# The value projection moved ahead of the key projection, and the key rotation's draining ticks set between query and key products of the recurrence

## The reference

```python
h = modulate(x, norm1_gain, sh1, sc1);  z = h @ w_in
gq, gk, gv, gr, glr, dq, dk, dv, gates = split(z)
# mixer A: gated linear attention, 4 heads, state 128 x 256, blocks of 16 tokens, decay from glr
# mixer B: differential attention, 8 heads; q and k: rmsnorm per 64 values, then rotary
qd = rope(rmsnorm(dq, q_gain), pos);  kd = rope(rmsnorm(dk, k_gain), pos);  v = dv
x = x + gt1 * ((sigmoid(g_a) * y_a + sigmoid(g_b) * y_b) @ w_out)
h2 = modulate(x, norm2_gain, sh2, sc2)
# PEER: per token 8 heads x 16 experts chosen by top-k of product keys among 16384
act = gelu(sum(h2 * peer_u[idx]));  x = x + gt2 * sum(g * act * peer_v[idx])
```

## Time and profile before

| | |
|---|---|
| median of three runs | 4257.27 us |
| profiled execution, its own time | 4264.31 us |
| its span | 4262.5 us |
| mean granted clock of TensorE | 0.802 |
| PE matmul / weight load / DVE / ACT / POOL busy | 73% / 47% / 64% / 35% / 29% |
| DMA | 1499.19 MB, mean 352 GB/s |

### The profile page before, as it was taken

One profiled execution on the slowest core, in us unless ns is written; L12 is line 12 of the kernel. 1 busy time (PEld: TensorE's weight loads), 2 busy tenths in 40 slices (PEclk: granted clock), 3 DMA queues, 4 the chain that ended last, 5 costly groups with the idle time before them and its releaser, 6 DMA issues. The chain is left out here.

```text
span 4262.5 us, 48896 instructions
## 1 busy us (share of the span) xinstructions
PE 3112.3 (73%) x15864; PEld 1989.7 (47%) x15864; DVE 2708.3 (64%) x7617; ACT 1513.0 (35%) x3085; POOL 1253.3 (29%) x1068
## 2 busy tenths in 40 slices
PE   6787688898788769788887679788776676633333
PEld 4676565676555327555554347454442364400000
DVE  1326357437667884578568874596678845776775
ACT  3533366312255651113555540133456611010010
POOL 0000112112233332333233332333333323354453
PEclk8798888899888779899878789888787788855555
DMA  7485767788989989999889899999999999999997
GB/s 263 142 323 188 285 237 260 270 312 336 361 342 373 359 313 398 394 417 404 352 353 361 335 368 385 414 399 400 382 387 383 373 414 413 396 415 415 414 404 329
DMA packets 269366, 1499.19 MB, mean 352 GB/s; under 512 B 44969, under 2 KB 81673, under 8 KB 97465
## 3 DMA queue, kind: packets, MB, share of 16 engines
q0 software_dynamic: 152064, 1107.36, 65.1%
q1 hardware_dynamic: 117048, 388.70, 24.2%
HBM read 1463.49 MB, written 31.36 MB: 351 GB/s over the span
## 5 line engine op out<-in xcount | busy, mean ns | idle before, releaser
L1711 POOL DMA_INDIRECT rt_ring<-in_peer_uv,rt_few_idx x1056 | 1250.0, 1184 | 2979.8 <-PE rt_acc L886 2344.6
L1657 DVE SCALAR_TENSOR_TENSOR rt_ring<-rt_ring,rt_h 128x1024 f32<-128x1024 f32 x1056 | 1267.6, 1220 | 541.2 <-DMA rt_ring<-in_peer_uv,rt_few_idx 536.6
L886 PE MATMUL rt_acc<-rt_ring,rt_diag 128*32 128x512 f32 x4224 | 762.4, 797 | 602.3 <-DVE rt_diag L1668 600.4
L635 PE MATMUL pair<-dense,w 128*128 128x256 f32 (+2 forms) x3056 | 599.4, 355 | 25.8 <-DMA w<-in_weights 24.2
L635 PEld LDWEIGHTS pair<-dense,w 128*128 128x128 f32 x3056 | 518.2, 198 | 140.7 <-issue 62.9
L624 PE MATMUL pair<-w,dense 128*128 128x256 f32 (+1 forms) x2352 | 557.8, 395 | 7.0 <-DVE dense L1313 2.8
L1212 ACT ACTIVATE rt_act_dot<-rt_dot 128x2 f32<-128x2 f32 x528 | 106.0, 202 | 1271.7 <-DVE rt_ring L1657 1262.5
L886 PEld LDWEIGHTS rt_acc<-rt_ring,rt_diag 128*32 128x32 f32 x4224 | 100.9, 122 | 930.1 <-DVE rt_diag L1668 789.3
L624 PEld LDWEIGHTS pair<-w,dense 128*128 128x128 f32 (+1 forms) x2352 | 437.5, 189 | 159.1 <-issue 73.7
L1668 DVE TENSOR_SCALAR rt_diag<-cst,rt_act_dot,rt_few_prob 128x32 f32<-128x32 f32 x1056 | 266.2, 297 | 82.6 <-ACT rt_act_dot L1212 64.1
L635 PE MATMUL bank<-dense,w 128*128 128x256 f32 (+2 forms) x1424 | 276.0, 350 | 1.4 <-DMA w<-in_weights 0.9
(11 more groups left out here) (241 smaller groups left out, 3314.5 us busy)
## 6 DMA issues: line engine op xcount, KB each, us to landing
w<-in_weights SPq DMA_DIRECT2D x284, 1024.0 KB
rt_ring<-in_peer_uv,rt_few_idx POOLq DMA_INDIRECT x1056
dense<-scratch_mod SPq DMA_DIRECT2D x18, 512.0 KB, 11.0
dense<-in_x_prompt SPq DMA_DIRECT2D x16, 512.0 KB, 10.3
rt_h<-scratch_h SPq DMA_DIRECT2D x33, 128.0 KB
rt_x<-scratch_x SPq DMA_DIRECT2D x132, 32.0 KB
out_k_prompt<-dense SPq DMA_DIRECT2D x32, 128.0 KB
out_v_prompt<-dense SPq DMA_DIRECT2D x32, 128.0 KB
```

The source lines that it names most:

```text
L635: mm = nc.tensor.matmul(bank[b][:, 0:n], wt[:, k * CH + j * P:k * CH + (j + 1) * P], src[:, k, 0:n], start=(k == 0), stop=(k == KC - 1))
L886: mm = nc.tensor.matmul(acc[u % 2][a * T:(a + 1) * T, :], diag[b % 2][:, i, :], slot[:, D + c * BANK:D + (c + 1) * BANK], start=(q == 0), ...
L1657: dt = nc.vector.scalar_tensor_tensor(up, up, 1.0, h2[u % 2][:], ALU.mult, ALU.mult, accum_out=dot[:, b % 2, i:i + 1])
L1711: nc.gpsimd.indirect_dma_start(ring[n % RING][:], None, d["peer_uv"], bass.IndirectOffsetOnAxis(ap=few_idx[u % 2][:, c:c + 1], axis=0)).th ...
```

## The change

From group 1 on, the `dv` ticks stand ahead of the `dk` ticks, and so do their weight blocks. The six draining ticks of `dk` no longer follow its eight products directly: four stand one behind each of the `gq` and `gk` products of the first pair of heads, the other two behind the last of them. The wait of TensorE for the normalised activations (`normed`) is made by whichever of the two stages starts. Group 0 keeps its order. The sum of costs of a group's ticks is unchanged; since the first 14 ticks of group 1 are now four of `norm` and ten of `dv`, `marks[0]` falls from 54 to 44.

```diff
--- before.py
+++ after.py
@@ -108,7 +108,7 @@
     names = []
     for part in range(2):
         names += [("mod", part, u) for u in range(4)] if g == 0 else []
-    for kind in ("dk", "dv"):
+    for kind in ("dk", "dv") if g == 0 else ("dv", "dk"):
         names += [(kind, i) for i in range(4)]
     for p in range(2):
         names += [("gq", p), ("gk", p), ("gv", 2 * p), ("gv", 2 * p + 1), ("gr", 2 * p), ("gr", 2 * p + 1)]
@@ -159,15 +159,26 @@
         for kind in ("modrow", "modcol"):
             out.extend(((kind, part), 0.5) for part in range(2))
     add("norm", nt + 2, 4.5)
-    for kind in ("dk", "dv"):
-        lag = 6 if kind == "dk" else 2
-        for i in range(4):
-            for ti in range(nt):
-                out.append(((kind, g, i * nt + ti), 3.6 if kind == "dk" else 3.0))
-        out.extend(((kind, g, 4 * nt + i), 1.0) for i in range(lag))
+    turns = []
+    if g == 0:
+        for kind in ("dk", "dv"):
+            lag = 6 if kind == "dk" else 2
+            for i in range(4):
+                for ti in range(nt):
+                    out.append(((kind, g, i * nt + ti), 3.6 if kind == "dk" else 3.0))
+            out.extend(((kind, g, 4 * nt + i), 1.0) for i in range(lag))
+    else:
+        out.extend((("dv", g, i), 3.0 if i < 4 * nt else 1.0) for i in range(4 * nt + 2))
+        out.extend((("dk", g, i), 3.6) for i in range(4 * nt))
+        turns = [(("dk", g, 4 * nt + i), 1.0) for i in range(6)]
     for p in range(2):
         for kind in ("gq", "gk"):
-            out.extend(((kind, g, p, j), 3.0) for j in range(2))
+            for j in range(2):
+                out.append(((kind, g, p, j), 3.0))
+                out.extend(turns[:1])
+                turns = turns[1:]
+        out.extend(turns)
+        turns = []
         out.extend((("la", g, p, j), 3.0) for j in range(3))
         out.extend((("gv", g, p, i), 3.0) for i in range(2 * nt))
         out.append((("gv", g, p, 2 * nt), 0.5))
@@ -637,14 +648,17 @@
                 mm.then_inc(bank_made[b], 1)
                 return bank_made[b], before + 1
 
+            def normed(g):
+                for t in GROUPS[g]:
+                    for i in range(2):
+                        b, before = sessions["n", t, i]
+                        pe.wait_ge(bank_free[b], before + 1)
+
             def rotary(kind, g, n):
                 nt = len(GROUPS[g])
                 among = ALL
                 if kind == "dk" and n == 0:
-                    for t in GROUPS[g]:
-                        for i in range(2):
-                            b, before = sessions["n", t, i]
-                            pe.wait_ge(bank_free[b], before + 1)
+                    normed(g)
                 if n < 4 * nt:
                     i, ti = n // nt, n % nt
                     at_end = tokens((kind, g, i, ti), weights((g, kind, i)), ti, hT, among)
@@ -662,6 +676,8 @@
 
             def dv(g, n):
                 nt = len(GROUPS[g])
+                if n == 0:
+                    normed(g)
                 if n < 4 * nt:
                     i, ti = n // nt, n % nt
                     released[g, "dv", i] = tokens(("dv", g, i, ti), weights((g, "dv", i)), ti, hT, ALL)
```

## The result

The changed kernel takes 4284.61 us (median of six runs, 4277.76 to 4295.05) against 4257.02 us before: ratio 1.0068, 95% interval 1.0052 to 1.0084. It is 27.6 us slower where 28 us faster were forecast. Its profiled execution took 4280.76 us, with a span of 4279.0 us. The two traces differ by 16.5 us, not 27.6: the one of before lies 7 us over its kernel's median, the one after 4 us under its own. What follows explains those 16.5 us and, by the batches, the lead that was lost on the way.

A forecast was written before the change was run, and what follows sets the result against it. From 455 to 1033 us TensorE was taken as nearly full, then the DMA engines, after a mixed fill. The terms -24 + 2 - 6 = -28 us, from a 4257.3 us median, gave 4229 us, range 4209 to 4251 us.

The forecast's parts named there:

- Part 1: Fill: rotations and scalings leave VectorE's path, so the first gather moves up some 9 us, between 7 and 12.
- Part 2: Group 1: TensorE no longer idles in front of batch 0, a gain of 24 us, bounds 12 and 33.8.
- Part 4: Group 2's stretch, 1033 to 1144 us: a gain of 6 us, between 0 and 16.
- Part 3: Draining ticks: ScalarE's third la tick waits for the kT store; 2 us loss in group 1, none elsewhere.
- The distance: Last kT store issued some 8 us, two to three ticks, ahead of ScalarE's third la tick.
- The landing: The last kT store takes 10.5 us to land in group 2 and 17.5 us in group 3.
- The cover: Where DMA is full, nine ring slots of 2.5 us (22 us) are on their way, so the engines go on.
- Rival D: Slower: ScalarE's kT store wait at the third la tick costs 38 us against 30 gained, 4265 us; chance 0.07.
- Part 5: Groups 3 and 4: DMA is full in their dk and dv stretches, so 0, bounds +3 and -3 us.

The follow-up runs named there:

- e3: Kernel before, keys still first, only the last three dk draining ticks set behind gq 0, gq 1 and gk 0: 4297.9 us, ratio 1.0088.
- e7: Kernel before with four instead of 14 ticks of group 1 in the fill, order unchanged: 4264.25 us, ratio 1.0013.
- e1: Changed kernel with two key staging tiles moved, so ScalarE needs no wait for the kT stores: 4233.37 us, ratio 0.9947 to the kernel before.
- e2: Changed kernel, values still first, with the six dk draining ticks directly behind their products: 4238.03 us, ratio 0.9952 to the kernel before.
- e6: Changed kernel with the new order for groups 1 and 2 only and e1's moved staging tiles: 4222.61 us, ratio 0.9909 to the kernel before.
- e8: Changed kernel with the kT stores issued by ScalarE behind its own copies instead of by SyncE: 4233.2 us, ratio 0.9943 to the kernel before.
- e9: e6 with the six dk draining ticks directly behind their products: 4234.69 us, ratio 0.9941 to the kernel before.
- e10: e6 with the kT stores issued by ScalarE too: 4215.86 us, ratio 0.9897 to the kernel before.

## Why the prediction was wrong

**Part 1 (first gather) was right in size, by two terms that were both too large.** 9 us forecast, 8.1 measured, or 9.9 when set against the first product, which in this trace starts 1.7 us later. The index load came 9.3 us earlier where 11.7 were forecast, and the gather followed it by 5.1 instead of 3.9 us: the block issued 3.3 us in front of it cost 1.2 us, not the 2.5 charged.

**Part 2 (group 1) was right in size, not in its reason.** 24 us forecast, 19.6 measured, with 10.1 us at the transposes where I had 7, and 4.8 us for the store where I had 2. But I priced TensorE's idle time as worth its length by itself. e3 takes that idle time away and gains nothing, because SyncE's list then brings the weights late; e7 brings the gather earlier and gains nothing. The lead needs both.

**Part 4 (group 2) was sized too low.** 6 us forecast of 0 to 16; 12.1 by batch 64, and 13.6 between batches 48 and 80 in e1 (9.9 to 16.3 in e2, e6, e8, e9 and e10). 111 - 13.6 = 97 us is close to the 95 us that the DMA bytes needed.

**Part 3 is the step that failed.** It charged 2 us in group 1 and none elsewhere, with bounds of 0 and 38 us; the waits are 66.1 us, and taking them away gives 51 us back (e1). It had the wait in view and sized its distance wrong, and it put the cost at nothing by a cover that isn't one:

- *The distance*, the largest term. "Some 8 us ahead of ScalarE's third `la` tick" counted ticks by TensorE's products. The store was issued 3.0, 3.3 and 1.3 us ahead of ScalarE's being ready, and in group 4 6.5 us behind. ScalarE has almost nothing in these ticks (4.4 us from the last copy to ready in group 2), and SyncE had a unit's loads in front of the store in groups 3 and 4. With 8 us of distance the four landings measured would have left 0, 19.6, 8.2 and 7.6 us, an estimate of 35 us in all, inside the bound of 38.
- *The landing.* 10.5 and 17.5 us are medians of four stores in the old place; the last of the four took 18.9, 18.7 and 12.2 us in groups 2 to 4 even there. In the new place it took 27.6, 16.2 and 15.6 us: 9 us longer in group 2, where it follows a weight block and two key rows stores at once, 3 us longer in group 4 and shorter in group 3. Part 1 had weighed a small load behind a block in one ring, and I didn't carry it to the store.
- *The cover.* "Nine ring slots of 2.5 us are on their way, so the engines go on" is true of the DMA engines during the wait (1.01) and false of the time. The ring is a loop: Gelu, diagonals, `weigh`, slot, gather. While ScalarE waits no slot comes back, GpSimd issues nothing for 30.9 us, and the gap comes out at the end (0.51 for 39 us, against 1.02 in e1). A buffer covers a wait only if the work can catch up afterwards, and here DMA is at its limit and can't.

**Rival D was the right one.** Its mechanism, place and the Gelu behind it are what the trace shows. It had 0.07, for two reasons: the wait's length was capped at 9.5 us, and the ring was credited as cover. With 17 us a group, D's own arithmetic gives 4257.3 - 30 + 66 = 4293 us against 4284.6 measured. Two errors partly cancel in that: without the wait the change gains 24.7 us, not 30 (e1), and the 66 us of waiting cost 51.

**Part 5** holds only roughly: no gain in groups 3 and 4, but a loss of some 8 to 11 us (e6 against e1, by the traces and by the medians), outside the bound of 3 us that I gave. Why stays open; VectorE waits 16.7 us for the store in e1 and 2.4 us in e6, which may be a part of it.

## What to carry to other kernels

When a step is moved later, list first what reuses its buffers and who waits for its stores to land; price that wait by the waiting engine's own list (what it still has to do in between), not by the pace of the engine that looks busiest, and look at what the issuing engine has in front of the store. Take a store's landing time from its new place in the order, behind whatever its issuer puts in front of it. In-flight transfers hide a stall from the DMA share while it lasts; look at the stretch behind it.

## What the runs showed of the hardware that was not expected

The same 256 KB store of 1 KB rows took 27.6 us from SyncE's ring behind 1.3 MB (a weight block and the key rows) and 12.4 us from ScalarE's, both with the DMA engines full (DMA share 1.01 from 1136 to 1161 us, and 1.03 from 1128 to 1141 us in e8). This is the largest of four differences (the others 0.1, 10 and 4 us). Issuing the stores from ScalarE cost a few lines and gave back 51 us of 4285 (e8).
